# DSA sample stage: low halves of the keys on VectorE, the choice laid out in three parts, a fifth place for pages; index stage: first pages gathered in the projection, score copy split

## What is computed

```python
dots = einsum('bqhd,bkd->bqhk', q_idx, k_idx)                 # 8 heads x 32
score = einsum('bqh,bqhk->bqk', w_idx, relu(dots))
score = where(key_pos <= pb[..., None], score, -inf)
_, sel = lax.top_k(score, 256)
s = einsum('bqhd,bqkd->bqhk', q, k[sel]) * 64 ** -0.5         # 8 heads x 64, one shared key/value head
p = softmax(where(valid, s, -inf)); out = p @ v[sel]
```

## Time and profile before

| | us |
|---|---|
| median of 3 runs | 3232.73 |
| the three runs | 3229.4 to 3234.01 |
| the profiled execution | 3235.45 |
| its span, first to last instruction | 3233.7 |
| TensorE busy | 2981.4 (92%) |
| VectorE busy | 1415.6 (44%) |
| ScalarE busy | 1001.1 (31%) |
| GpSimd busy | 641.2 (20%) |
| mean granted clock of TensorE | 0.963 of full |

### The profile page before, as it was taken

How to read it: one execution, slowest core, us unless ns; L and a number is a source line. 1 busy time by engine, 2 the same in 40 slices (tenths; PEclk the granted TensorE clock), 3 DMA queues, 4 the chain that set the end, 5 groups by cost and what they waited for, 6 DMA issues and landing times. The chain is left out here.

```text
span 3233.7 us, 45582 instructions
## 1 busy us (share of the span) xinstructions
PE 2981.4 (92%) x18298; PEld 2554.9 (79%) x18298; DVE 1415.6 (44%) x2116; ACT 1001.1 (31%) x1612; POOL 641.2 (20%) x562
## 2 busy tenths in 40 slices
PE   7999999778898889999999999996888988999997
PEld 7999879655576679998799997784656666999975
DVE  2222264468763352222532223644877444322236
ACT  2121233444442232212321222334444433211223
POOL 1111031221122141110221110411302132311103
PEclk9999999889898999999999999997999989999998
DMA  4222452300122332223432224513001233222243
GB/s 117 83 78 78 139 162 63 130 1 1 66 84 95 111 98 78 78 84 131 156 87 83 78 91 144 157 33 131 1 17 66 84 111 129 74 80 82 87 142 126
DMA packets 241737, 293.79 MB, mean 91 GB/s; under 512 B 12624, under 2 KB 205488, under 8 KB 235456
## 3 DMA queue, kind: packets, MB, share of 16 engines
q1 hardware_dynamic: 234688, 229.00, 23.0%
q0 software_dynamic: 6912, 62.92, 5.3%
HBM read 287.72 MB, written 3.88 MB: 90 GB/s over the span
## 5 line engine op out<-in xcount | busy, mean ns | idle before, releaser
L159 DVE TENSOR_TENSOR wlo<-raw,whi 128x1024 fp32r<-128x1024 f32 (+2 forms) x398 | 514.6, 1294 | 1295.4 <-ACT whi L153 1294.3
L153 ACT ACTIVATE whi<-raw 128x1024 fp32r<-128x1024 f32 (+2 forms) x398 | 418.5, 1053 | 1435.7 <-PE ps L608 864.6
L608 PE MATMUL ps<-xth,whi 128*128 128x296 f32 x2624 | 752.1, 299 | 5.4 <-PEq L770 5.4
L608 PE MATMUL ps<-xtl,whi 128*128 128x296 f32 x2624 | 754.6, 300 | 0.0
L608 PE MATMUL ps<-xth,wlo 128*128 128x296 f32 x2624 | 571.7, 300 | 0.0
L608 PEld LDWEIGHTS ps<-xth,whi 128*128 128x128 f32 x2624 | 494.6, 188 | 5.5 <-issue 5.5
L608 PEld LDWEIGHTS ps<-xtl,whi 128*128 128x128 f32 x2624 | 493.3, 188 | 0.0
L608 PEld LDWEIGHTS ps<-xth,wlo 128*128 128x128 f32 x2624 | 427.5, 188 | 0.0
L166 PE MATMUL ps<-whi,hth 128*128 128x512 f32 (+1 forms) x880 | 350.6, 398 | 10.0 <-DVE wlo L159 8.4
L168 PE MATMUL ps<-whi,htl 128*128 128x512 f32 (+1 forms) x880 | 346.9, 394 | 0.0
L167 PE MATMUL ps<-wlo,hth 128*128 128x512 f32 (+1 forms) x880 | 346.8, 394 | 0.0
(11 more groups left out here) (402 smaller groups left out, 4423.2 us busy)
## 6 DMA issues: line engine op xcount, KB each, us to landing
raw<-in_ffn_w_in SPq DMA_DIRECT2D x176, 512.0 KB, 3.8
raw<-in_ffn_w_out SPq DMA_DIRECT2D x176, 512.0 KB, 3.5
raw<-in_w_o SPq DMA_DIRECT2D x32, 512.0 KB, 3.3
raw<-in_w_in SPq DMA_DIRECT2D x16, 507.0 KB, 3.9
gb<-in_ln_g SPq DMA_DIRECT2D x6, 512.0 KB, 5.4
gb<-in_ln_b SPq DMA_DIRECT2D x6, 512.0 KB, 6.3
raw<-in_w_in SPq DMA_DIRECT2D x8, 338.0 KB, 3.9
x<-in_x_prompt SPq DMA_DIRECT2D x1, 1536.0 KB, 10.8
```

The costliest lines, as they stand in the source:

```text
L153: e.activation(dst, T.raw[:, s, 0:width], ACT.Copy).then_inc(S.hi_done, 1)
L159: e.tensor_tensor(w_lo, T.raw[:, s, 0:width], w_hi.bitcast(F32), ALU.subtract).then_inc(S.split_done, 1)
L608: mm = e.matmul(bank(u, up)[:, h, :], part[:, s, w], xp[:, k, o], start=(k == 0 and part is T.whi and xp is T.xth), stop=(k == KD - 1 and ...
```

## The change

Index stage and projection: the gathers of rows 0 and 1 are issued by GpSimd in the projection, behind the four memsets and ahead of the copies into sB. `high(0)` goes ahead of `new_relu` on ScalarE, `low(0)` ahead of the new tokens' scores on VectorE. The first two pads are zeroed and filled in the index stage. The score copy is split by PSUM bank: VectorE takes one half, ScalarE the other.

Prompt stage: two memsets of pads on GpSimd in place of four, no pad copies on ScalarE, no `pe_keys`.

D stage: `low` moves from GpSimd to VectorE, row 0 ahead of all else, row 2p+1 in slot 2, row 2p+2 in slot 5. `high(2p+2)` moves from slot 6 to slot 4. `choice_out` is cut into one half after chunk 1, the other after chunk 2, and the new keys' part in slot 2. A fifth place, `pg4`, lies over `score`, so row 4 is gathered once the choice is laid out (`bias_set` 4). Rows 5, 6, 7 go to places 0, 1, 2, and each waits for the values of row 0, 1, 2. GpSimd keeps only gathers. The M stage keeps its order.

```diff
 # projection, GpSimd
             for q in (T.QI, T.QP, T.QA, T.QB):
                 e.memset(q[:, :, :].bitcast(F32), 0.0).then_inc(S.stack_zero, 1)
+            e.wait_ge(S.w_used, B + NW)
+            for r in range(2):
+                page_load(e, T, r, T.ip[r][:, :, :], W["cache_dsa"], r)
             e.wait_ge(S.sa_done, 2)
 # index stage, GpSimd
-            for r in range(DEC_B):
-                if r >= 2:
-                    e.wait_ge(S.kl_done, r - 1)
+            for pad in pads[0:2]:
+                e.memset(pad[:, :], 0.0).then_inc(S.pads_zero, 1)
+            for r in range(2, DEC_B):
+                e.wait_ge(S.kl_done, r - 1)
                 page_load(e, T, r, ip[r % 2][:, :, :], cache_dsa, r % 2)
 # index stage, end: ScalarE (half 1) and VectorE (half 0)
+            e.wait_ge(S.pads_zero, 2)
+            for pad, rows in ((pads[0], slice(32, 64)), (pads[1], slice(96, 128))):
+                for to, of in pad_copy(pad, T.kcT, rows):
+                    e.activation(to, of, ACT.Copy)
+            e.wait_ge(S.weighed, DEC_B // 2)
+            score_out(e, 1, cp)
...
-            e.tensor_copy(T.score[:, 0:HPAST].rearrange("t (p i) -> t i p", i=PAGES),
-                          flat[:, 4 * 512:4 * 512 + HPAST].rearrange("t (i p) -> t i p", i=PAGES))
+            score_out(e, 0, e.tensor_copy)
 # prompt stage, TensorE and VectorE
-                    if i == 0:
-                        e.wait_ge(S.pe_keys, 4)
...
-            e.wait_ge(S.pads_zero, 4)
+            e.wait_ge(S.pads_zero, 2)
 # places of the pages
+SLOTS = [[r % 2 for r in range(DEC_B)], [r % 4 for r in range(DEC_B)], [0, 1, 2, 3, 4, 0, 1, 2]]
 # D stage, GpSimd
+                for r in (2, 3):
+                    pages(r)
+                e.wait_ge(S.bias_set, 4)
+                pages(4)
+                for r in range(5, DEC_B):
+                    values_done((r - 5) // 2, (r - 5) % 2)
+                    pages(r)
 # sample stages, ScalarE
-                    if p + 1 < PAIRS and j == 6:
+                    if p + 1 < PAIRS and j == (6 if M else 4):
                         high(2 * p + 2)
 # D stage, VectorE
             if not M:
-                choice_out()
+                low(e, 0)
             chunk_out(e, 0, "D")
             for p in range(PAIRS + 1):
                 for j in range(8):
                     if turned_in(p, j) is not None:
                         chunk_out(e, turned_in(p, j), "D")
+                    if not M and p == 0 and j < 2:
+                        choice_out(j)
+                    if not M and p < PAIRS and j == 2:
+                        low(e, 2 * p + 1)
+                    if not M and p == 0 and j == 2:
+                        choice_new()
+                    if not M and p + 1 < PAIRS and j == 5:
+                        low(e, 2 * p + 2)
```

More of the change, by code:

```diff
@@ L881, in proj_tensors @@
     T.score_at = A.top + 16384
+    T.pads = [T.M.put(f"pkeys{i}", [P, PROMPT], F32, T.score_at + 2 * HKEYS * 4 + i * PROMPT * 4) for i in range(2)]
+    T.pg4 = T.M.put("pg4", [P, PAGES, ROW], F32, T.score_at)
+    assert T.score_at + PAGES * ROW * 4 <= T.arena + 2 * KF * TOK * 4
     T.sI = T.M.put("sI", [SAMPLE, IH, P], F32R, A.top + 16384)
@@ L889, in proj_tensors @@
     assert A.top <= T.arena + 2 * KF * TOK * 4, A.top - T.arena
+    T.ip1_at = T.xth_at + 3 * PAST * 4
+    T.ip = [T.M.put(f"ip{i}", [P, PAGES, ROW], F32, at) for i, at in enumerate((T.hi_at, T.ip1_at))]
     T.sA = T.M.put("sA", [SAMPLE, AH, P], F32R, T.xth_at)
@@ L1471, in sample_step, with pad_copy @@
         e.match_replace(T.swork[:, :], best, left[:, :], TAKEN).then_inc(S.s_round_done, 1)
+def pad_copy(pad, src, rows):
+    return [(pad[rows, c:c + w], src[rows, k0:k0 + w]) for c, k0, w in ((0, 0, S0), (S0, TAIL, PROMPT - S0))]
 def prompt_block(nc, T, S, next_cache):
@@ L1521, in prompt_block @@
     tail = T.score_at + 2 * HKEYS * 4
-    assert tail % 64 == 0
-    pads = [T.M.put(f"pkeys{i}", [P, PROMPT], F32, at_) for i, at_ in
-            enumerate((tail, tail + PROMPT * 4, T.QI_at, A.region(PROMPT * 4)))]
+    pads = T.pads + [T.M.put(f"pkeys{i}", [P, PROMPT], F32, at_) for i, at_ in ((2, T.QI_at), (3, A.region(PROMPT * 4)))]
     Q4 = Map(T.nc, tail + 2 * PROMPT * 4)
@@ L1602, in k_at @@
         return pad[:, k0:k0 + w]
-    def pad_copy(pad, src, rows):
-        return [(pad[rows, c:c + w], src[rows, k0:k0 + w]) for c, k0, w in ((0, 0, S0), (S0, TAIL, PROMPT - S0))]
     def keys(t):
@@ L1626, in _ @@
         def _(e):
-            for pad in pads:
+            for pad in pads[2:4]:
                 e.memset(pad[:, :], 0.0).then_inc(S.pads_zero, 1)
@@ L1791, in _ @@
         def _(e):
-            e.wait_ge(S.pads_zero, 2)
-            for pad, rows in ((pe_keys[0], slice(32, 64)), (pe_keys[1], slice(96, 128))):
-                for dst, src in pad_copy(pad, T.kcT, rows):
-                    e.activation(dst, src, ACT.Copy).then_inc(S.pe_keys, 1)
             def mix_hi(q, kind, t):
@@ L1940, with pages_there @@
 INDEX_SEMS = ["w_zero", "w_set", "kh_done", "kl_done", "turned", "out_act", "out_dve", "dots_done", "relu_done", "weighed",
-              "new_dots", "new_relu", "new_weighed", "scored"]
-PAGE_SEMS = ["page_in0", "page_in1", "page_in2", "page_in3"]
-INDEX_FILLS, SAMPLE_FILLS = DEC_B // 2, DEC_B // 4
-def pages_there(e, T, l, stage, slot, fill):
-    index = INDEX_FILLS if slot < 2 else 0
-    a_layer = index + 2 * SAMPLE_FILLS
-    before = 0 if stage == 0 else index + (stage - 1) * SAMPLE_FILLS
-    e.wait_ge(T.page_in[slot], l * (16 * a_layer) + 16 * (before + fill + 1))
+              "new_dots", "new_relu", "new_weighed", "scored", "pads_zero"]
+PAGE_SEMS = ["page_in0", "page_in1", "page_in2", "page_in3", "page_in4"]
+SLOTS = [[r % 2 for r in range(DEC_B)], [r % 4 for r in range(DEC_B)], [0, 1, 2, 3, 4, 0, 1, 2]]
+def pages_there(e, T, l, stage, r):
+    slot = SLOTS[stage][r]
+    a_layer = sum(slots.count(slot) for slots in SLOTS)
+    before = sum(slots.count(slot) for slots in SLOTS[:stage]) + SLOTS[stage][:r].count(slot)
+    e.wait_ge(T.page_in[slot], l * (16 * a_layer) + 16 * (before + 1))
 def page_load(e, T, r, dst, cache, slot):
@@ L1985, in index_block, with score_out @@
     jobs = [(r, g) for r in range(DEC_B) for g in range(4)]
+    pads = T.pads
+    def score_out(e, half, copy):
+        h = PAGES // 2
+        copy(T.score[:, 0:HPAST].rearrange("t (p i) -> t i p", i=PAGES)[:, half * h:(half + 1) * h],
+             T.ps[:, 4 + half, :].rearrange("t (i p) -> t i p", i=h))
     def freed(e, q):
@@ L2097, in _ @@
                                 ALU.mult).then_inc(S.w_set, 1)
+            low(0)
             e.wait_ge(S.new_weighed, 1)
@@ L2100, in _ @@
             e.tensor_tensor(T.score[64:P, HPAST:HKEYS], T.ps[64:P, 4, 0:DEC_T], T.tri8[64:P, :], ALU.add).then_inc(S.scored, 1)
-            low(0)
             low(1)
@@ L2136, in sample_block @@
     C1.region(4 * PAGES * ROW * 4)
-    pg = T.pg
+    slots = [T.pg[:, i, :, :] for i in range(4)]
+    if not M:
+        slots.append(T.pg4[:, :, :])
+    pg = [slots[i] for i in SLOTS[1 if M else 2]]
     olS = T.M.put(n + "olS", [P, DEC_B, BH, DEC_T], F32, C1.region(2048))
@@ L2263, in _ @@
                                 base=0, pattern=[[1, P]], channel_multiplier=-1).then_inc(S.ones_set, 1)
-            for r in range(1, 4):
-                low(r)
-            for r in range(4, DEC_B):
-                values_done(r // 2 - 2, r % 2)
-                page_load(e, T, r, pg[:, r % 4, :, :], cache, r % 4)
-                low(r)
+                for r in range(1, 4):
+                    low(e, r)
+                for r in range(4, DEC_B):
+                    values_done(r // 2 - 2, r % 2)
+                    pages(r)
+                    low(e, r)
+            else:
+                for r in (2, 3):
+                    pages(r)
+                e.wait_ge(S.bias_set, 4)
+                pages(4)
+                for r in range(5, DEC_B):
+                    values_done((r - 5) // 2, (r - 5) % 2)
+                    pages(r)
             if M:
@@ L2461, in high @@
             def high(r):
-                pages_there(e, T, l, stage, r % 4, r // 4)
+                pages_there(e, T, l, stage, r)
                 if r >= 2:
```

50 lines of the change are left out of this document (25 added, 25 removed).

## The result

| | before | after |
|---|---|---|
| median of the runs | 3232.86 us | 3203.3 us (3197.86 to 3205.96) |
| ratio | | 0.9908, 95% interval 0.9891 to 0.9925 |
| profiled execution | 3235.45 us, span 3233.7 us | 3204.29 us, span 3202.4 us |
| granted clock, mean | 0.963 | 0.972 |

The change took 29.6 us off the median and 31.3 us off the span of the profiled execution. Measured again in a later session, beside parts of itself, the same kernel ran in 3206.24 us against 3230.28 us: ratio 0.9928, interval 0.9914 to 0.9943. So the gain is 24 to 30 us, and the last few microseconds of it are not settled by either measurement.

What follows compares the result with a forecast made beforehand. TensorE, busy 92% of the span, bounds the kernel; gains come only where it stands still or runs at lower clock. 13.6 + 1.8 + 1.9 + 12.9 = 30.2 us gave a forecast median of 3203 us, range 3194 to 3216 us.

Steps and rivals of the forecast that it cites:

- Index stage, start: Head of both index stages: pages gathered early let TensorE turn sooner and row 3 come earlier, 13.6 us together.
- row 3: Index stage of layer 0: its high half comes at 608.8 us, 7.4 us gained; 6.2 us in layer 1.
- Cover in the projection (term 0): End of projection: two gather issues, 2.4 us, fit GpSimd's 2.87 us idle time; 2.2 us of QL delay covered.
- Index stage, end: Score copy after the last product, split over VectorE and ScalarE: 0.95 us per half, 1.8 us gained in both layers.
- Prompt stage, start: Pads at the prompt stage's head: two memsets, not four, start VectorE 0.97 us earlier, 1.9 us in both layers.
- D stages: Both DSA sample stages: shorter head and gaps between pairs, 91.8 us each, 12.9 us gained together.
- first gap: D stage, between pairs 0 and 1: scores go on 3.25 us after pair 0 instead of 4.2 us.
- the case of the full clock: Rival, D stages: the clock stays full, 5 us more gain, 3198 us; chance 0.80 together with the forecast.
- the bound of 89.5 us: Lower bound for a D stage's length, at full clock with an estimated 16.8 us a pair.
- VectorE as bound: Rival, D stages: 16 low halves cost 0.8 us each on the path, gain 17.3 us, 3215 us; chance 0.08.
- Mutual blocking of the low halves: Rival, D and index stages: VectorE's low halves and GpSimd delay each other 2.06 us each time, 3243 us; chance 0.03.
- Early pages that don't pay: Rival, projection and index stage: gathers hold QL back or land late, gain 16.6 us, 3216 us; chance 0.06.

Runs made afterwards that it cites:

- the D part alone: Only the D stages' changes kept, projection, index and prompt edits taken back from the changed kernel: 3219.16 us, ratio 0.9967.
- the early part: Only early pages, early pad copies and divided score copy kept, D stages as in the kernel before: 3217.28 us, ratio 0.9965.
- four places: Changed kernel with four D-stage page places, and the next pair's high and low halves in later slots from pair 1 on: 3206.68 us.
- index stage reordered: Changed kernel with weights written by GpSimd, VectorE's low halves first, new keys weighed later, ScalarE copies ahead of the ReLU, pads zeroed later: 3202.98 us.
- every low half twice: Changed kernel with a second VectorE instruction of the same form ahead of each D-stage low half: 3219.65 us.
- the high half late: Changed kernel, five places kept, next pair's high half back after chunk 6 and the low half one slot behind: 3212.53 us, ratio 0.9943.

## Why the prediction was right, and where its steps were not

The forecast was 3203 us with 30.2 us of gain against the profiled execution; its span went down by 31.3 us and the median is 3203.3 us. That is closer than the terms deserve, and partly luck: two of them missed in opposite directions, and the repeat gave only 24 us, 23.3 us by its ratio with an interval of 18 to 28 us, which leaves the 30.2 us out. In that session the D part alone gave 10.7 us (12.9 predicted) and the early part 11.3 us (7 to 16 us by its interval, 17.3 predicted).

- **Index stage, start (predicted 13.6 us).** By the start of the ReLU of the last pair the stages gained 6.5 and 5.4 us, 11.8 us; 0.6 us went at the stop ahead of the stage, so 11.3 us. Undoing it alone cost 9.5 us. The first turn came 9.74 - 4.13 = 5.6 us earlier within the stage (predicted 5.95 us). The failing step is row 3: placed at 608.8 us with 7 us of landing, it came at 611.08 us after 9.15 us. With both first pages there, low(0) and low(1) follow each other at once, so the issues of pages 2 and 3 came 1.5 us apart (600.41 and 601.93 us) where the kernel before had 3.1 us between them, and the second came no sooner for it. By the landings in the trace the page of row 3 came 4.3 and 3.3 us behind that of row 2, where it had been 4.5 and 3.1 us in the kernel before. So row 3 gained only about what row 2 gained, 5.7 and 5.4 us, and not the 7.4 us and 6.2 us predicted: a landing time counted from the issue was the wrong measure with another gather under way.
- **Cover in the projection (term 0).** Held: sB, QL and the last transposes came no later. But the barrier behind them took longer, which the prediction took for fixed.
- **Index stage, end (1.8 us).** 1.02 and 1.01 us in place of 1.86 us: 1.7 us in both layers. Held, from an assumed ScalarE row.
- **Prompt stage, start (1.9 us).** From the end of the score copy to the first maximum 6.14 to 5.42 us and 6.41 to 5.09 us: 2.0 us. Held.
- **D stages (12.9 us).** 16.6 us in the profiled execution, 15.1 us in the D part alone. The later gaps were 2.4 us to the tenth, the first turn 1.8 us earlier (1.7 predicted). For the first gap the prediction's own rows give 3.1 us (1015.2 less 0.5, plus 1.6, less 1013.2), not 3.25 us; measured were 3.1 and 2.6 us. The size was off in the pairs, 17.4 us against 16.5 to 16.6 us in five of six: this was the case of the full clock, which the range held, and its 16.8 us a pair was near. The stage of 90.0 us lies close to the bound of 89.5 us.
- **What carries it.** Here the reasoning was half right. It counted 1.7 us at the head for low halves off GpSimd and put the borders down to the fifth place. By the runs the engine of the low halves and the order of the choice are worth nothing (89.7 and 90.0 us), and the slot of the high half, which the prediction mentioned only as a consequence, carries the larger part that a run could take back: with the old slot at all three borders 4 us of gap a stage came back, 5 us in the pairs, and 5 to 11 us in the median. How this divides over the borders is open, since the old slot at the last two of them, and four places with it, cost only 0.5 to 2 us in the median. The fifth place is what lets the high half go early at these borders, and it covers a late page: with four places a page that landed after 8.8 us made a gap of 6.2 us, one that landed after 6.3 us a gap of 3.7 us.

The rivals: VectorE as bound fell (48.4 of 90.0 us busy, 0.9 us to spare at the borders) except in the head, where it was true and worth 3.5 us a stage. Mutual blocking of the low halves fell: all 16 took 1.21 to 1.23 us with GpSimd keeping only gathers, and even with GpSimd's arithmetic back, one collision a stage cost nothing in the kernel's time. It held the gathers up by 2.1 us where GpSimd's small work stood ahead of them (index stage reordered). Early pages that don't pay fell: taken back, they cost 9.5 us.

## What to carry to other kernels

Where an engine prepares work for the next round, find the slot in each queue at which the preparation no longer stands in the way of the current round's reductions; a buffer more is worth having when it frees that slot, and which engine does the work may not matter. Ahead of moving small work to an idle GpSimd, look for what is queued behind it there, gathers above all, and for two-input VectorE work beside it. On TensorE's path look at a stop twice: as idle time, and for the clock at which the work behind it goes. Judge by medians: the profiled executions here lay up to 8 us off theirs.

## What the runs showed of the hardware

**The clock went with small differences.** In the changed kernel stops of 1.48 us between pairs went with a granted clock of 1.00 in the pairs; with 1.81 to 1.88 us (every low half twice) the pairs went at 0.90 and took 1.2 us more each. It is no rule of one stop's length: with four places, stops of 0.37 and 2.27 us stood ahead of a pair at 1.00, and with the high half late a gap of the same 3.7 us stood ahead of one at 0.84. What decides it was not settled here.

**The stop at a stage border grew with gathers ahead of it.** Without the early gathers TensorE's stop ahead of the index stage was 1.96 to 2.00 us in six stages of three kernels; with them it was 2.00 to 2.82 us in 22 stages of eleven profiled executions, on average 2.54 us in layer 0 and 2.24 us in layer 1. The cause is open: no run issued other gathers there, or the same ones earlier.

**A page lands some microseconds behind the one before it.** A gather 3.1 us behind the one before landed 7.7 and 6.6 us after its issue (kernel before, row 3, layers 0 and 1), one 1.5 us behind it after 9.15 and 8.3 us. In all 28 index stages profiled, row 3 landed 2.9 to 4.6 us after row 2, whether it was asked for 1.3 or 3.6 us behind it. Row 2, asked for at least 7.6 us behind row 1, took 6.2 to 6.8 us in 27 of them. The neighbour is not all: in a D stage (four places, row 4) a gather asked for 27 us behind the one before took 8.8 us, and why is open.
